# Dilated keys of the decode cache scored by GpSimd products and VectorE sums instead of TensorE

## The reference, cut to what matters

```python
DIL_PAIRS = ((128, 1), (512, 4), (2048, 16))
...
for g, (window, dil) in enumerate(DIL_PAIRS):
    idx = qi - dil * jnp.arange(window // dil + 1)[None, :]
    o, lse = gathered_attention(q[:, :, g * DIL_KV_HEADS:(g + 1) * DIL_KV_HEADS], k_ext, v_ext, idx)
```

## Time and profile before

| | |
|---|---|
| Median of 3 runs | 1296.88 us (1294.82 to 1299.54) |
| Profiled execution | 1295.6 us, its span 1293.7 us |
| PE busy | 1230.6 us (95%) |
| DVE busy | 401.1 us (31%) |
| ACT busy | 245.5 us (19%) |
| POOL busy | 34.8 us (3%) |
| DMA | 499.18 MB, q1 busy 94.4% of 16 engines' span |

### The profile page before, as it was taken

One profiled execution on the slowest core, in us unless ns is written; L12 is line 12 of the kernel. 1 busy time (PEld: TensorE's weight loads), 2 busy tenths in 40 slices (PEclk: granted clock), 3 DMA queues, 4 the chain that ended last, 5 costly groups with the idle time before them and its releaser, 6 DMA issues.

```text
span 1293.7 us, 15236 instructions
## 1 busy us (share of the span) xinstructions
PE 1230.6 (95%) x6402; PEld 529.3 (41%) x6402; DVE 401.1 (31%) x909; ACT 245.5 (19%) x487; POOL 34.8 (3%) x47
## 2 busy tenths in 40 slices
PE   8999999999999999999999999999999999899996
PEld 4456667767443333333333333323333333333332
DVE  2244553314434223132231322222131313222233
ACT  2212434312121101121011210101110121101012
POOL 0000004200200000000000000000000000000000
PEclk9999999999999999999999999999999999999998
DMA  8999848889899999999999999999999999999994
GB/s 289 362 368 329 324 163 288 286 251 420 312 355 372 430 429 428 426 427 429 428 429 428 427 428 428 428 428 427 429 428 427 429 429 427 428 428 428 429 427 190
DMA packets 71673, 499.18 MB, mean 386 GB/s; under 512 B 5952, under 2 KB 29120, under 8 KB 45984
## 3 DMA queue, kind: packets, MB, share of 16 engines
q1 hardware_dynamic: 70752, 495.79, 94.4%
q0 software_dynamic: 848, 2.36, 0.6%
HBM read 495.27 MB, written 36.96 MB: 411 GB/s over the span
## 4 chain that ended last, share of the span: by engine, by line
PE 64%; DMA 32%; DVE 2%; ACT 1%; issue 1%; SPq 0%; DVEq 0%; ACTq 0%
DMA ring<-in_w_gate_up 20%; PE ps L1731 19%; PE ps L1770 10%; PE ps L1194 7%; DMA late<-in_w_gate_up 6%; PE ps L1110 5%; PE ps L1687 3%; DMA tail<-in_w_gate_up 3%; PE ps L1631 3%; PE ps L1481 2%; PE ps L1494 2%; PE ps L1748 1%; PE ps L1342 1%; PE ps L1172 1%; PE ps L1359 1%; PE ps L1650 1%
## 5 line engine op out<-in xcount | busy, mean ns | idle before, releaser
L1731 PE MATMUL ps<-ring,cq 128*64 128x512 f32 x1232 | 282.2, 599 | 22.0 <-DMA ring<-in_w_gate_up 21.9
L1731 PEld LDWEIGHTS ps<-ring,cq 128*64 128x64 f32 x1232 | 84.1, 137 | 194.5 <-issue 144.7
L1770 PE MATMUL ps<-ring,cq 128*64 128x512 f32 x592 | 134.3, 595 | 0.7 <-issue 0.7
L994 ACT ACTIVATE cq<-ps 128x512 f32<-128x512 f32 x32 | 19.1, 597 | 450.8 <-PE ps L1748 450.8
L1194 PE MATMUL ps<-arena,ring 128*128 128x288 f32 x384 | 102.3, 412 | 2.1 <-ACT ring L838 2.1
L2239 DVE TENSOR_REDUCE tail<-ps 128x1 f32<-128x288 f32 x15 | 6.9, 458 | 289.6 <-PE ps L1663 289.6
L1194 PEld LDWEIGHTS ps<-arena,ring 128*128 128x128 f32 x384 | 69.6, 189 | 25.6 <-issue 4.9
L1110 PE MATMUL ps<-ring,arena 128*128 128x512 f32 (+3 forms) x240 | 72.3, 555 | 2.3 <-DMA ring<-in_w_in 2.3
L1770 PEld LDWEIGHTS ps<-ring,cq 128*64 128x64 f32 x592 | 41.0, 136 | 73.3 <-issue 69.8
L2267 DVE TENSOR_TENSOR x_tok<-x_tok,ps 64x512 f32<-64x512 f32 (+2 forms) x51 | 43.9, 861 | 67.4 <-PE ps L1687 61.9
L1008 ACT ACTIVATE cq<-ps 64x512 f32<-64x512 f32 x32 | 18.9, 591 | 230.1 <-PE ps L1770 230.1
(11 more groups left out here) (376 smaller groups left out, 1295.7 us busy)
## 6 DMA issues: line engine op xcount, KB each, us to landing
ring<-in_w_gate_up SPq DMA_DIRECT2D x77, 2048.0 KB, 42.2
ring<-in_w_down SPq DMA_DIRECT2D x37, 2048.0 KB, 43.9
tail<-in_w_gate_up SPq DMA_DIRECT2D x13, 2048.0 KB, 40.6
late<-in_w_gate_up SPq DMA_DIRECT2D x12, 2048.0 KB, 41.9
cq<-in_w_gate_up SPq DMA_DIRECT2D x12, 2048.0 KB, 42.4
arena<-in_w_gate_up SPq DMA_DIRECT2D x12, 2048.0 KB, 42.6
ring<-in_w_in SPq DMA_DIRECT2D x9, 2048.0 KB, 9.1
out_dil_k_s<-in_cache_dil_k SPq DMA_DIRECT2D x8, 2044.0 KB
```

The lines of the kernel that those rows point to most:

```text
L994: act_e.activation(xTe if isinstance(b, int) and b == NE - 1 else aTe, bank(4)[:, :].rearrange("p (q m) -> p q m", m=P), ACT.Copy).then_in ...
L1731: ins = pe.matmul(bank(gu0 + u)[64 * h:64 * h + 64, :], xTe[:, k % 4, (k // 4) * 64:(k // 4) * 64 + 64], pair_buf[slot][:, a:a + 512], sta ...
L1770: ins = pe.matmul(bank(7 if last else 5)[64 * h:64 * h + 64, :], aT[:, kk % 4, (kk // 4) * 64:(kk // 4) * 64 + 64], pair_buf[slot][:, a:a ...
```

## The change

The keys of the strided groups no longer go through TensorE.

- Queries: after the rotation, GpSimd writes the 32 decode rows of the two strided groups' queries (512 values each) to a DRAM buffer `q_rows`, waits, and reads them back in 8 DMAs so that in `q_rep[b]` each partition p holds the queries of token p mod 4 of sequence b.
- Keys: `load_dilated_keys(b)` loads 7 blocks in 7 DMAs into one of two slots (8 KiB per partition), so ordered that partition p holds rows of residue p mod 4. Of the recent rows 128 are also needed for stride 16: their product goes to an eighth block.
- Products: GpSimd multiplies keys by queries in place, in 4 instructions per sequence (256, 768, 512 and 512 elements per partition).
- Sums: VectorE's `sum_keys(b)` sums 64 elements at a time (2048 elements per partition to 32) into `sT`. The eight sums stand behind `unit_norm` of units 1, 2, 4, 5, 7, 8, 10 and 11. `load_dilated_keys(b)` for b from 2 on waits for `k_sum` of b-2.
- After the last sum, VectorE spreads the sums in 8 copies of 128x128 into rows (`s_rows`), and TensorE transposes these 8 blocks into the scores' place.
- What stays on TensorE per sequence: the last 128 rows of branch B (stride 1), A and C, loaded by `load_dot_keys(b)` in 3 DMAs into five slots. That is 7 transposes instead of 19 and 16 products instead of 28. These 128 rows are loaded twice, in both layouts. TensorE waits for all eight sums before the first key transpose.
- The windows of queries for all sequences are made in two ScalarE instructions before the prompt's units; before, two instructions per sequence stood between the products.
- Values: five slots instead of four, 9 DMAs per sequence instead of 6; the first three sequences' values are issued as soon as the eighth sum is done.

```diff
+            pool.wait_ge(S["rope_done"], 5)
+            pool.dma_start(d["q_rows"], q_tok[0:NS, 2, 768:1280]).then_inc(S["q_out"], 16)
...
+            for b in range(NB_S):
+                pool.wait_ge(S[f"cache{b % 2}_in"], 16 * 7 * (b // 2 + 1))
+                k = k_dil[b % 2].rearrange("p (c n) -> p c n", n=256)
+                q4, q16 = q_rep[b][:, 0:256], q_rep[b][:, 256:512]
+                pool.tensor_tensor(k[:, 0, :], k[:, 1, :], q16, ALU.mult).then_inc(S["near_done"], 1)
+                pool.tensor_tensor(k[:, 5:8, :], k[:, 5:8, :], q16.unsqueeze(1).to_broadcast([P, 3, 256]), ALU.mult)
+                pool.wait_ge(S["near_done"], b + 1)
+                for half in range(2):
+                    c = slice(1 + 2 * half, 3 + 2 * half)
+                    ins = pool.tensor_tensor(k[:, c, :], k[:, c, :], q4.unsqueeze(1).to_broadcast([P, 2, 256]), ALU.mult)
+                ins.then_inc(S["k_mul"], 1)
...
+            def sum_keys(b):
+                v.wait_ge(S["k_mul"], b + 1)
+                v.tensor_reduce(sT[:, 32 * b:32 * b + 32], k_dil[b % 2].rearrange("p (c n) -> p c n", n=HD), AX.X, ALU.add) \
+                    .then_inc(S["k_sum"], 1)
+            SUMS_BEHIND = (1, 2, 4, 5, 7, 8, 10, 11)
...
                 unit_norm(u)
+                if u in SUMS_BEHIND:
+                    sum_keys(SUMS_BEHIND.index(u))
...
+            pe.wait_ge(S["k_sum"], NB_S)
             k_transposes(0)
+            pe.wait_ge(S["qw_ready"], 1)
...
+            pe.wait_ge(S["rows_ready"], 1)
+            for c in range(8):
+                at = (c - 1) * P if c else 896
+                pe.transpose(SP[:, at:at + P], s_rows[:, c, :], ident)
...
+            def load_values(b):
+                s, sm = vslot[b % NVS], val_in[b % NVS]
+                if b < 3:
+                    sp.wait_ge(S["k_sum"], NB_S)
+                elif b < NVS:
+                    sp.wait_ge(S["s_scores_done"], 1)
+                else:
+                    sp.wait_ge(S["s_pv_done"], b - NVS + 1)
```

More of the change, by code:

```diff
@@ L250, in build @@
         pair_in = [sem(f"pair{k}_in") for k in range(NSLOT)]
+        dot_in = [sem(f"dot{k}_in") for k in range(len(k_dot))]
+        val_in = [S["cache0_in"], S["cache1_in"]] + [sem(f"val{k}_in") for k in range(2, NVS)]
         block = es.enter_context(nc.Block())
@@ new lines, in far_rows, with load_dilated_keys @@
+            def far_rows(src):
+                return src[0:1536].rearrange("(r q s) n -> r q s n", r=3, s=16)[:, :, 0:4, :]
+            def load_dilated_keys(b):
+                s, sm = k_dil[b % 2], S[f"cache{b % 2}_in"]
+                if b >= 2:
+                    sp.wait_ge(S["k_sum"], b - 1)
+                src = d["cache_dil_k"][0, b].rearrange("r h n -> r (h n)")
+                for r in range(4):
+                    sp.dma_start(s[:, 256 * (1 + r):256 * (2 + r)], recent_rows(src)[r]).then_inc(sm, 16)
+                for r in range(3):
+                    sp.dma_start(s[:, 256 * (5 + r):256 * (6 + r)], far_rows(src)[r]).then_inc(sm, 16)
@@ L569, in _ @@
             sp.dma_start(cst[:, P:], d["consts"][:, P:]).then_inc(S["cst_in"], 16)
-            for i in range(1, 9):
+            for i in range(1, 8):
                 load_wblk(i)
@@ L588, in _ @@
                     .then_inc(S["copy_dma"], 16)
-            for i in range(3, 8):
-                load_cache(i)
             copy_cache()
-            for i in range(8, 12):
-                load_cache(i)
+            for b in range(5, NB_S):
+                load_dot_keys(b)
+            copy_cache()
+            load_values(3)
+            load_values(4)
             load_wblk(12)
-            for i in range(12, 16):
-                load_cache(i)
+            for b in range(5, NB_S):
+                load_values(b)
             load_wblk(13)
@@ L920, in _ @@
             for b in range(NB_S):
[L921 to L930 removed]
+                evict_kt(act_e, b, 1, lambda o, i: act_e.activation(o, i, ACT.Copy), "kta_evicted")
             evict_gate()
@@ L1358, in add @@
                     half = slice(64 * r, 64 * r + 64)
-                    return pe.matmul(out, qw[half, r, chunk, win], rhs[half], start=start, stop=last, skip_group_check=True)
-                def crossed(part, h):
-                    m, r = h // 2, h % 2
-                    row = slice(32 * (2 * m + 1 - r), 32 * (2 * m + 1 - r) + 32)
-                    if part == 0:
-                        return add(SC_C[row, :], r, 10 + m, kTs[:, 1920 + m * LM:1920 + (m + 1) * LM], first)
-                    return add(SC_A[row, part - 1, :], r, 2 * m + part - 1, kTs[:, 896:1024], False)
@@ L1368, in _ @@
-                for part in range(4):
+                    return pe.matmul(out, qwin[half, chunk, win], rhs[half], start=start, stop=last, skip_group_check=True)
+                for part in range(3):
                     for h in range(4):
                         m, r = h // 2, h % 2
-                        row = slice(32 * h, 32 * h + 32)
-                        kb = kTs[:, m * 1024:m * 1024 + 896]
+                        row = slice(32 * (2 * m + 1 - r), 32 * (2 * m + 1 - r) + 32)
                         if part == 0:
-                            own = add(SP[row, 0:512], r, 6 + m, kb[:, 0:512], first)
-                            crossed(0, h)
-                        elif part == 1:
-                            crossed(1, h)
-                            own = add(SP[row, 512:896], r, 8 + m, kb[:, 512:896], first)
-                            crossed(2, h)
-                        elif part == 2:
-                            own = add(SP[row, 896:1024], r, 8 + m,
-                                      kb[:, 0:512].rearrange("p (a s) -> p a s", s=16)[:, :, 0:4], False)
-                        else:
-                            own = add(SP[row, 1024:1152], r, 4 + m, kb[:, 384:512], first)
@@ L1385, in _ @@
-                own.then_inc(S["s_scores_b"], 1)
+                            add(SP[32 * h:32 * h + 32, 1024:1152], r, 4 + m, kTs[:, m * P:(m + 1) * P], first)
+                            add(SC_C[row, :], r, 6 + m, kTs[:, 384 + m * LM:384 + (m + 1) * LM], first)
+                        else:
+                            ins = add(SC_A[row, part - 1, :], r, 2 * m + part - 1, kTs[:, 256:384], False)
+            pe.wait_ge(S["rows_ready"], 1)
+            for c in range(8):
+                at = (c - 1) * P if c else 896
+                pe.transpose(SP[:, at:at + P], s_rows[:, c, :], ident)
```

196 lines of the change are left out of this document (107 added, 89 removed).

## The result

The changed kernel takes 1320.62 us in the median of four runs (1318.04 to 1322.91), beside 1296.35 for the kernel before on the same chip: a ratio of 1.0183, 95% interval 1.0156 to 1.0211. That is 1.8% slower, where I had forecast 0.65% faster, and outside my range. The profiled execution has a span of 1316.2 us, 22.5 more than before.

A forecast was written before the change was run, and what follows sets the result against it. TensorE was taken to bound the front, a fixed amount of expert weights the rest. 1295.6 - 20.8 (key stage) + 7 (prompt attention) + 5.5 (last keys) = 1287.3, or 1288.5 on the median's scale, 0.65% less; range 1278 to 1302.

The forecast's parts named there:

- Bound of the front: Before the expert stream: TensorE bounds the front and releases the weight loads, so a microsecond saved there moves everything by one.
- The cached keys on TensorE: TensorE's key stage in decode attention: 18.5 us instead of 39.3, so 20.8 us less.
- The queries' trip: Queries through DRAM from the rotation on: more than 20 us until the first keys can be there, so no cost.
- VectorE in prompt attention, the term of 7 us: TensorE late by 7 us at the end of prompt attention through VectorE's sums and GpSimd's products; bounds 2 and 24.
- my upper bound of 24: Prompt attention: TensorE's lateness if each round of the key loop needs 24 us, with the eighth sum at 216.
- The sums' part: VectorE in prompt attention: eight sums of 2.3 us, most of their 18.4 us hidden if products are in time.
- a bound of 28 us: Prompt attention: all three instructions of a normalization wait for GpSimd's port lock, at most 28 us less the slack.
- The loop of keys: Two key slots in prompt attention: a round of 17 to 18 us nearly fits 17.3; fifth keys land at 168 to 172.
- The last keys, 5.5 us: TensorE's key stage: sixth sequence's keys land near 229.5, wanted at about 224, so some 5.5 us wait (0 to 9).
- Rival 1: Prompt attention: the key loop with GpSimd decides once a round takes over about 22 us; 10 us slower, 1307; 16%.
- my own sign: Prompt attention: products over 6 us, or VectorE idle before the sums over 15 us in total, means the loop rival holds.
- Rivals 2 and 3: 2: attention and last keys hide everything, 1278, 15%. 3: 3 MB more in DMA-bound experts, 1296.9, at worst 1300, 10%.

The follow-up runs named there:

- run 4: Changed kernel with the last three sequences' other keys issued ahead of gate block 11 and the copies; 1309.8 us, ratio 1.011.
- 7: Changed kernel, nothing left out, SP's issue order alone rewritten (copies later, fifth strided and last other keys earlier); 1301.0 us, ratio 1.003.
- 14: Reordered kernel with the products on VectorE instead of GpSimd, and SP's order fitted to that; nothing left out; 1292.9 us, ratio 0.996.
- run 2: Changed kernel with the three cache copies behind gate block 7 moved behind the fifth sequence's keys; 1312.8 us, ratio 1.013.
- 3: Changed kernel without the queries' trip through DRAM, replicated queries filled with ones, copies left in place; 1310.0 us, ratio 1.012.
- run 6: Changed kernel with all transfers, but products and sums shrunk to tiny copies; 1303.0 us, ratio 1.005.
- run 10: Changed kernel with VectorE's sums only: no strided key loads, no queries' trip, no GpSimd products; 1294.0 us, ratio 0.998.
- run 5: Changed kernel with products and sums on data in memory, without strided key loads and queries' trip; 1308.3 us, ratio 1.008.
- run 11: Changed kernel with SP's order rewritten, two cache copies now ahead of the first values, products still on GpSimd, nothing left out; 1285.1 us, ratio 0.990.

## Why the prediction was wrong, point by point

- **Bound of the front: right.** From the start of values to the end of the span it took 1029.8 us before, 1030.3 in the changed kernel and 1030 to 1031 in all runs but 4, 7 and 14, which waited for later values.
- **The cached keys on TensorE: right.** 17.8 us against 18.5 forecast, without the wait.
- **The queries' trip "hidden": wrong.** Its last two reads landed at 137 to 139 us, behind the time at which I had the first keys (128). A DMA of GpSimd's queue stood 17.6 us in issue, and its transfers and three copies stood before the first keys. The trace has 7.9 to 13.0 us to landing for its four reads of 448 KB, beside other transfers. The Trainium skill (DMA: Bandwidth & Descriptors, "Anatomy of one DMA — SWDGE (gpsimd) path") gives 2.0 us and the bytes by 436 GB/s for one DMA, which makes an estimate of 3.1 us for 448 KB. The trace does not agree, and it decides. Runs 2 and 3 show this cause, and run 6 its size with the keys' own transfers: 13.0 us.
- **VectorE in prompt attention, the term of 7 us: the step that failed.** It measured 25.5; even my upper bound of 24 was below that. The sums' part was right (0.8 us in run 10). The port's part is 14.8 us alone. I had a bound of 28 us for it from three waits in each of eight sequences, but the count that gave the 7 us had GpSimd's and VectorE's instructions at their undisturbed lengths, so it stood in the sum at nothing. I had also counted three instructions of branch B and overlooked that the units of branch A have five that can wait, and that with products back to back each waits again. I had also weighed VectorE's idle half as cover; it is none for a chain of short dependent instructions. And I had not priced the clock that falls behind a wait.
- **The loop of keys: half right.** The fifth keys were late behind block and copy, as said, but their products began 13 to 17 us later than I had their landing. The distance from block to landing was right (155 to 168 or 172 forecast, 169.01 to 184.80 measured), but the block waits for TensorE, itself 13 us late by then, and the keys for the third sum, at 169.76. In run 2, where the first wait was 4.3 us, the block went out at 155.76 and the products began at 172.10. The terms of my round add up to 15.1 us; for the 2 to 3 us of semaphores on top I had no row. From the end of the first sum to that of the third it took 21.2: 4.8 for issue, 3.0 for landing, 5.9 for products, 5.2 until VectorE came to the sum, and 2.3.
- **The last keys, 5.5 us: mis-sized, 18.0.** The mechanism is shown by run 4. From eighth sum to keys I had 31 us (198.5 to 229.5); it took 41 (217.3 to 258.2): issues of values 17.5, behind them 3.5 to the first of these keys, 1.2 more to the sixth sequence's memory keys, and 18.7 for these to land. TensorE began the stage 14.3 us behind the eighth sum (14.5 forecast), so these 10 us are wait, and 2.3 more since it wanted the keys 8.7 and not 11 us into the stage.
- **Rivals.** Rival 1 named the right place and the right sign, and priced it at 1307. By my own sign it holds: VectorE's idle time before the sums is 12.93 + 5.88 = 18.8 us, over 15. But 12.93 of it is the first sum, which no round precedes, and before the third sum the products were ready 5.2 us early. So its mechanism was only half of it: a round of the loop is not what decides, as run 5 has no loads and loses 15.5 us, and run 11 keeps both slots and all loads and is faster than before. Rivals 2 and 3 fell.

## What to carry to other kernels

Work given to GpSimd is not free for VectorE where VectorE's chain is of short instructions with SBUF operands and TensorE waits for its end: each of them can wait for a whole GpSimd instruction (0.65 to 1.19 us instead of 0.16 here). Ask first whether VectorE itself has the time; here it did the same products in half the time (2.6 us a sequence instead of 4.9), with TensorE's waits as before the change (1.4 us). And a path with small transfers that somebody waits for must be written into the queue ahead of bulk ones, one bulk transfer at a time between them: rewriting the order of SP's issues alone, with GpSimd's products left as they were, took the change from 1.8% slower to 1.0% faster.

## What the hardware showed that I had not expected

- An issue on SP's queue was held 9 to 14 us (10.97, 9.07, 14.25) when keys or values and copies of 2 MiB were in flight ahead, so everything written behind it was late too. On GpSimd's queue the seventh of eight DMAs stood 17.6 us, and 8.3 with three copies fewer.
- TensorE's wait of 13.2 us left the granted clock at 0.50 of full speed (1.2 GHz) behind it as well: 1.97 us for eight transposes instead of 1.03.
- GpSimd's products were lengthened too: 3.48 us for the pair of 512 instead of 2.48, in run 5, with a VectorE product of two SBUF operands (2.04 us instead of 1.23) beside it.
